# Differential attention: TensorE turns the probability tiles ahead of a step's scores instead of behind them

## The reference, cut to what matters

```
# q, k: (S, 4 heads, 2, 64); v: (S, 4 heads, 128)
sc = einsum('cbhqd,cbhkd->cbhqk', q * 64**-0.5, k) + bias   # two score maps per head
p  = softmax(sc, axis=-1)
a  = p[0] - lam * p[1]
o  = einsum('bhqk,bhkv->bhqv', a, v)
# then rms_norm(o) * gain, times silu(gate)
```

## Time and profile before

| what | value |
|---|---|
| time before, median of 3 runs | 3135.67 us (3135.11 to 3137.91) |
| time of the profiled execution | 3137.64 us |
| its span, first to last instruction | 3135.6 us |
| TensorE busy | 2688.3 us, 86% of the span |
| VectorE busy | 2014.8 us, 64% |
| ScalarE busy | 1569.2 us, 50% |
| GpSimd busy | 1150.6 us, 37% |
| mean granted TensorE clock | 0.928 of full |

### The profile page before, as it was taken

The page is one execution under the profiler, slowest core; times in us unless marked ns, Lnnn a source line. Parts: engine busy times, 40 slices in busy tenths (PEclk is TensorE's granted clock), DMA queues, the critical chain, the costliest instruction groups (busy, mean ns, idle before and its releaser), DMA issues. The chain is left out here.

```text
span 3135.6 us, 41536 instructions
## 1 busy us (share of the span) xinstructions
PE 2688.3 (86%) x14032; PEld 2108.9 (67%) x14032; DVE 2014.8 (64%) x4318; ACT 1569.2 (50%) x3035; POOL 1150.6 (37%) x981
## 2 busy tenths in 40 slices
PE   6999788699979997886989796997889696997887
PEld 5877566477868775664767575775667584775666
DVE  4472387588534723875984447988766448897666
ACT  3221266588432213765883315675763316675761
POOL 0100177365001002774650000984841001983831
PEclk9999899899989998998999899998999898998899
DMA  4443210100324431101013110210022110110022
GB/s 122 119 139 100 82 39 8 41 1 21 122 70 118 144 88 35 40 8 41 1 35 127 64 31 8 57 48 27 1 87 101 57 24 24 48 44 24 1 88 81
DMA packets 90751, 181.94 MB, mean 58 GB/s; under 512 B 12552, under 2 KB 27912, under 8 KB 90504
## 3 DMA queue, kind: packets, MB, share of 16 engines
q1 hardware_dynamic: 74124, 150.69, 15.1%
q10 hardware_dynamic: 16416, 28.61, 3.1%
HBM read 149.87 MB, written 33.33 MB: 58 GB/s over the span
## 5 line engine op out<-in xcount | busy, mean ns | idle before, releaser
L696 PE MATMUL ps<-w_hi,hh 128*128 128x512 f32 (+1 forms) x640 | 243.0, 380 | 22.2 <-DVE w_lo L581 10.1
L1251 POOL TENSOR_SCALAR a_prob<-a_prob,a_ratio 128x1024 f32<-128x1024 f32 x64 | 72.0, 1125 | 508.5 <-DVE a_ratio L1210 508.5
L696 PE MATMUL ps<-w_hi,hl 128*128 128x512 f32 (+1 forms) x640 | 240.3, 375 | 0.0
L696 PE MATMUL ps<-w_lo,hh 128*128 128x512 f32 (+1 forms) x640 | 239.7, 375 | 0.0
L1678 PE MATMUL ps<-o_w_hi,hh 128*128 128x512 f32 x512 | 211.5, 413 | 24.3 <-DVE o_w_lo L1602 24.3
L2141 DVE TENSOR_SCALAR_CACHE_REDUCE select_rows<-masks,select_cuts 128x1024 bf16<-128x1024 int16 (+7 forms) x264 | 229.3, 871 | 0.2
L1678 PE MATMUL ps<-o_w_lo,hh 128*128 128x512 f32 x512 | 207.3, 405 | 0.0
L1678 PE MATMUL ps<-o_w_hi,hl 128*128 128x512 f32 x512 | 206.1, 402 | 0.0
L948 POOL TENSOR_SCALAR b_prob<-b_prob,b_recip 128x1024 f32<-128x1024 f32 x128 | 144.2, 1127 | 162.5 <-DVE b_recip L907 160.0
L1658 POOL TENSOR_TENSOR o_rstd<-o_rstd,nhalf 128x1 f32<-128x1 f32 x56 | 46.6, 833 | 411.1 <-DVE o_rstd L1539 238.0
L1199 DVE CUSTOM_DVE_ANT_0 a_prob<-ps,a_bias 128x1024 f32<-128x1024 f32 x128 | 151.6, 1222 | 61.2 <-PE ps L1336 57.6
(11 more groups left out here) (354 smaller groups left out, 7920.2 us busy)
## 6 DMA issues: line engine op xcount, KB each, us to landing
w_early<-in_w_in SPq DMA_DIRECT2D x108, 256.0 KB, 2.8
ada_w<-in_w_ada ACTq DMA_DIRECT2D x96, 256.0 KB, 2.7
w_raw<-in_w_in SPq DMA_DIRECT2D x84, 256.0 KB, 2.8
xcur<-aq SPq DMA_DIRECT2D x16, 512.0 KB, 3.8
y<-xcur SPq DMA_DIRECT2D x16, 512.0 KB, 3.7
a_bias<-bias_tiles SPq DMA_DIRECT2D x8, 960.0 KB, 5.0
bq<-in_w_out SPq DMA_DIRECT2D x12, 512.0 KB, 3.8
closing_rows<-in_w_out SPq DMA_DIRECT2D x12, 512.0 KB, 4.3
```

Source lines behind the costliest of these rows:

```text
L696: mm = nc.tensor.matmul(o, lhs, rhs, start=(k == 0 and i == 0), stop=(k == K - 1 and i == 2))
```

## The change

On TensorE the attn turns of a step go ahead of its scores; only the nat turns stay at the end of the step. The table is filled with the attn elements first, so that in the steps that hold both kinds they also come first in `order`, and with it in the banks and in the read-outs of ScalarE and VectorE. The other engines' loops are as they were.

```diff
     plan = {g: [] for g in range(START, END + 1)}
-    for h in range(A_HEADS):
-        plan[T * h - 1 if h else START] += [("nat", h, w, e) for w in range(2) for e in range(HALF)]
     for n in range(NSB):
         for j in range(T):
             plan[QB * n + 6 + j // 2].append(("attn", n, j))
+    for h in range(A_HEADS):
+        plan[T * h - 1 if h else START] += [("nat", h, w, e) for w in range(2) for e in range(HALF)]
...
                 for g in range(START, END + 3):
                     for e in plan.get(g - 2, []):
                         product(e)
+                    for e in plan.get(g, []):
+                        if e[0] == "attn":
+                            turn(e)
                     if 0 <= g < NB:
                         scores(g)
                     if due(g, 12) is not None:
                         mean(due(g, 12))
                     if due(g, 14) is not None:
                         widen(due(g, 14))
                     for e in plan.get(g, []):
-                        turn(e)
+                        if e[0] == "nat":
+                            turn(e)
```

## The result

The changed kernel takes 3236.16 us as the median of four runs (3233.72 to 3239.07), the kernel before 3136.53 us beside it: a ratio of 1.0326, with a 95% interval from 1.0311 to 1.0341. The forecast was 3236 us.

What follows compares the result with a forecast made beforehand. The prediction saw TensorE full in a 4.1 us step, VectorE's read-outs covered by scores. The profiled 3137.6 us plus 82 (serial waits) and 18 (lower clock) gave 3238, less 2 for the median: 3236 us; eight in ten, 3206 to 3282.

Steps and rivals of the forecast that it cites:

- The chain: Plain step: shift, read-outs, turns and scores run one after the other, 6.2 us against 4.12 us.
- a weight load of scores pulled ahead: TensorE between turns and scores: an early weight load might be hidden, taking off some 0.1 us a step, 5 us in all.
- The middle stretch: scores(6) to scores(31): plain, lo-part and nat intervals sum to 179.3 us a layer, before the lower clock's 9 us.
- nat intervals: Intervals 7, 15 and 23, which hold nat turns: 13.2 us each, 39.6 us a layer.
- The clock term: Some steps run at TensorE's lower clock level behind the gap: 9 us a layer, +18 us for both.
- In front: Start of the stretch: turn(6) now stands before scores(6), 0.85 us each layer, 1.7 us in all.
- Behind scores(31): Tail of each layer: TensorE's order of work stays as before, so no change in time.
- fits into 6.2 with room: GpSimd's 4.2 us of work a step fits the longer step, so waits for its combined tiles and diagonals go.
- Most steps at the lower clock: Rival: same serial waits, with the lower clock level in most steps, 3270 to 3290 us; chance 0.13.
- Part of the chain covered: Rival: early turn release or lighter GpSimd load makes a step cost 5.4 us, 3200 us in all; chance 0.06.
- The change does nothing: Rival: scores pass the waiting turns or the wait is never met, 3136 us; chance 0.03.
- Read-outs under the scores: Rival: take(g) runs while VectorE waits for scores, TensorE's 4.0 us bounds a step, about 3130 us; chance 0.03.

Runs made afterwards that it cites:

- readouts_ahead: Changed kernel with ScalarE and VectorE reading out the attn turns of step g ahead of shift(g), not a step later: 3157.32 us, 1.0063.
- the narrow pair: VectorE's lo-part subtraction cut to 128 of 512 columns after the first four elements: 3197.92 us in the changed kernel, 3136.33 us in the kernel before.
- products_twice: Changed kernel with each product's three matmuls issued twice: 3238.41 us, 1.0325.
- tail_undone_b: Changed kernel with the turns behind mean and widen again in the steps behind the last scores: 3244.84 us, 1.0338.
- turns_before_mean: Kernel before with mean and widen moved behind all turns of the step, scores still first: 3129.38 us, 0.9977; repeated, 3129.65 us.
- narrow_rest_before: Kernel before with VectorE's lo-part subtraction cut to 128 of 512 columns after the first four elements: 3136.33 us, 1.0001.

## Why the prediction was right, point by point

- **The chain** is as it was written: 2.68 + 1.28 + 0.05 + 0.59 + 1.70 = 6.30 us, predicted 6.2. (The steps of the earlier trace rows are numbered one too high, there and in the prediction: 412.07 is the start of scores(9), and the two shifts are those of steps 8 and 9. No term hangs on it.) Only the term from the turn's release to scores was off, 0.59 for 0.41 us (and 0.08 allowed for): from the release of a bank's four transposes it took 0.59 us to scores and 0.41 to products. The 0.1 us a step that the prediction allowed for a weight load of scores pulled ahead is not there: at 476.33 the first weight load of scores starts with the first matmul. readouts_ahead and the narrow pair show the chain to be the cause, not only the place.
- **The middle stretch** was predicted at 179.3 + 9 = 188.3 us a layer and took 189.3 and 190.0. By terms: plain steps 0.1 us each too low, 2 us a layer; nat intervals 38.2 and 38.5 us for 39.6, though singly they ran from 11.4 to 14.2 where one price of 13.2 was taken; the lo part's own interval 7.43 for 7.3.
- **The clock term.** 9 us a layer was predicted. Taking 6.30 and 7.43 us off the 22 intervals of each layer leaves 9.1 and 9.5 us. That it is this close is chance: it was picked between 0 and 35 from two rows that disagreed. products_twice shows that the gap makes it, but for interval 6, which stays long there (7.57 and 8.29 us).
- **In front,** turn(6) was to cost 0.85 us in the stretch scores(0) to scores(6). The change there is +0.2 and +1.2 us, where steps at either clock level differ by more than that from one execution to the next. Interval 5, which holds the turn, shows the price better: 6.27 and 7.13 us, where other steps with scores at the lower level take 5.40. That is 0.87 us, and 1.73 in the second layer, where the transposes ran at the lower level too. Turn(6) also waited 2.34 and 3.45 us for GpSimd's first combined tiles, nearly all of it while shift(5) ran.
- **The step that failed** is "Behind scores(31) the order of TensorE's work is as before, so nothing". The attn turns also pass mean and widen there, and I looked only at their place to scores. It is worth 3.3 us a layer; tail_undone_b has it back, and turns_before_mean shows that it comes in full only behind the long steps. Left out of the sum, it offsets the too low plain step.
- **GpSimd,** "fits into 6.2 with room", is right for the changed kernel, and the reason why its lateness came out only in the experiments with steps of 4 us.
- **The rivals.** Most steps at the lower clock: no, 0.88 of full speed in the middle stretch. Part of the chain covered, steps of 5.4 us: no, 6.30. The change does nothing: no, scores did not pass the turns. Read-outs under the scores: not in this kernel, but made true by hand they gave 3157 us and, with the edits of three more runs, 3132. I had priced it at 3130 without the wait for the combined tiles.

That the forecast met the median to the microsecond is luck in the sum: the tail's -6.6 us and the terms above it cancel.

## What to carry to other kernels

When two engines hand work to and fro in a step, ask of every instruction that moves what is now queued behind its wait: a turn that waits for a read-out is harmless behind the scores and costs a third of the step in front of them. The price is a sum along one loop of waits, and from one undisturbed step of the trace it came out 0.1 us under the 6.30 measured. Where that loop was slower than the fullest engine, more work on that engine was free in the plain steps; where it got faster, the next engine's lateness, here GpSimd's, appeared. Work that waits for a slow engine and that nobody needs soon, as widen here, goes behind what others wait for.

## What the runs showed of the hardware

A VectorE instruction of four columns with two operands in SBUF took 1.83 to 1.87 us instead of 0.15 in two intervals a layer, and ended within 0.03 us of a GpSimd addition over SBUF that had started before it; VectorE's subtractions with one operand in PSUM kept their 1.28 us a pair beside the same GpSimd instructions. All traces in which VectorE makes the square bear it out: of 192 squares in twelve traces not one ended ahead of a GpSimd instruction that had started before it, and 46 took over 0.2 us. In narrow_rest_before ten of sixteen took 0.91 to 0.92 us, which cost nothing there, since VectorE had the room. The Trainium skill, SBUF — State Buffer, SBUF: two separate sides, says that the two engines share a pair of ports that is an exclusive lock for a whole instruction, for which a VectorE operation in a two-port mode, or one with two SBUF inputs against a GpSimd operation that reads SBUF, competes. The rows agree with it. The price was not only the 1.7 us of the instruction: with the granted clock that fell behind the gap, four such instances were worth 13 us in the rows of the two traces.

The granted clock fell behind gaps of 1.88 us in some steps and not in others of the same kernel, and no longer in the plain steps once the gap was 0.5 us. What decides between two equal gaps was not tried.
